# A two-layer mixture-of-experts network: expert 0's rows made by one-hot products

## What is computed

```python
def _moe(x, w_router, router_bias, w_gate, w_up, w_down):
    h = x.reshape(-1, D_MODEL)
    scores = jax.nn.sigmoid(h @ w_router)
    biased = scores + router_bias
    ...                      # the best of 4 groups, and in it the best 2 experts of each token: idx
    wts = jnp.take_along_axis(scores, idx, axis=-1)
    wts = wts / wts.sum(-1, keepdims=True)
    gates = jnp.sum(jax.nn.one_hot(idx, N_EXPERTS) * wts[..., None], axis=1)
    y = jnp.zeros_like(h)
    for e in range(N_EXPERTS):
        he = jax.nn.silu(h @ w_gate[e]) * (h @ w_up[e])
        y = y + gates[:, e:e + 1] * (he @ w_down[e])
    return y
# the layer's output: _layernorm(ALPHA * x + _moe(x, ...), g, b)
```

## Time and profile before

| | us |
|---|---|
| median of 3 runs | 1484.63 (1483.34 to 1486.12) |
| the profiled execution: time | 1496.51 |
| its span | 1494.8 |
| PE matmul busy | 1253.4 (84%) |
| DVE busy | 548.5 (37%) |
| ACT busy | 320.2 (21%) |
| POOL busy | 162.6 (11%) |

### The profile page before, as it was taken

One profiled execution on the slowest core, in us unless ns is written; L12 is line 12 of the kernel. 1 busy time (PEld: TensorE's weight loads), 2 busy tenths in 40 slices (PEclk: granted clock), 3 DMA queues, 4 the chain that ended last, 5 costly groups with the idle time before them and its releaser, 6 DMA issues.

```text
span 1494.8 us, 19415 instructions
## 1 busy us (share of the span) xinstructions
PE 1253.4 (84%) x7442; PEld 758.3 (51%) x7442; DVE 548.5 (37%) x1419; ACT 320.2 (21%) x776; POOL 162.6 (11%) x200
## 2 busy tenths in 40 slices
PE   1999992999972999999998499989997975999940
PEld 0486442454431577778876245546664533454420
DVE  1281354111115357855655334432111362111127
ACT  0101121111111232333332034422220121111111
POOL 0010003000002000012100600004400011000030
PEclk9999995999995999999997679999787986999975
DMA  9238028999924211000000810005403058999642
GB/s 378 80 147 206 0 89 321 380 364 367 349 108 160 113 57 57 0 15 4 3 3 1 255 44 1 1 9 153 137 19 141 1 207 332 353 365 367 260 159 80
DMA packets 68710, 227.56 MB, mean 152 GB/s; under 512 B 7713, under 2 KB 34401, under 8 KB 51969
## 3 DMA queue, kind: packets, MB, share of 16 engines
q1 hardware_dynamic: 41360, 140.95, 26.0%
q0 software_dynamic: 17440, 66.12, 12.7%
q10 hardware_dynamic: 9808, 19.14, 3.5%
HBM read 186.90 MB, written 39.29 MB: 151 GB/s over the span
## 4 chain that ended last, share of the span: by engine, by line
PE 80%; DVE 9%; DMA 6%; issue 3%; ACT 1%; POOL 0%; POOLq 0%; DVEq 0%; SPq 0%; ACTq 0%
PE bank L1152 15%; PE bank L1093 9%; PE bank L1172 7%; PE bank L1298 7%; PE bank L1222 4%; PE bank L1395 3%; PE bank L1240 2%; PE bank L1631 2%; PE bank L1644 2%; PE bank L1653 2%; PE bank L1633 2%; DMA xT<-in_xT_dram 2%; PE bank L1142 2%; DVE acc L2188 2%; PE bank L1583 2%
## 5 line engine op out<-in xcount | busy, mean ns | idle before, releaser
L1093 PE MATMUL bank<-ring,cat 128*128 128x512 f32 (+1 forms) x320 | 143.6, 604 | 9.0 <-DMA ring<-in_stream_dram 7.6
L1152 PE MATMUL bank<-ring,work 128*128 128x512 f32 x256 | 113.9, 597 | 0.0
L1298 PE MATMUL bank<-xT,ring 128*128 128x288 f32 x448 | 110.9, 407 | 0.0
L1093 PEld LDWEIGHTS bank<-ring,cat 128*128 128x128 f32 (+1 forms) x320 | 57.2, 183 | 83.3 <-issue 83.2
L1298 PEld LDWEIGHTS bank<-xT,ring 128*128 128x128 f32 x448 | 84.6, 190 | 24.1 <-issue 1.5
L2168 DVE TENSOR_TENSOR work<-work,bank 128x256 f32<-128x256 f32 x32 | 13.5, 421 | 219.0 <-ACT work L1753 219.0
L1152 PEld LDWEIGHTS bank<-ring,work 128*128 128x128 f32 x256 | 47.9, 192 | 54.2 <-issue 54.2
L1142 PE MATMUL bank<-const,work 128*128 128x128 f32 x256 | 36.1, 290 | 32.9 <-DMA work<-xrows 32.9
L1240 PE MATMUL bank<-ring,xT 128*128 128x512 f32 (+1 forms) x80 | 36.5, 618 | 32.0 <-DMA xT<-in_xT_dram 32.0
L1222 PE MATMUL bank<-xT,ring 128*128 128x288 f32 x256 | 63.1, 407 | 0.0
L1081 PE MATMUL bank<-const,x 128*128 128x128 f32 (+1 forms) x120 | 17.6, 299 | 50.4 <-DVE x L2004 50.4
(11 more groups left out here) (417 smaller groups left out, 2191.5 us busy)
## 6 DMA issues: line engine op xcount, KB each, us to landing
ring<-in_stream_dram SPq DMA_DIRECT2D x71, 1024.0 KB, 8.0
cat<-in_stream_dram SPq DMA_DIRECT2D x16, 1024.0 KB, 8.8
work<-xrows ACTq DMA_DIRECT2D x32, 512.0 KB, 4.9
xT<-in_stream_dram SPq DMA_DIRECT2D x16, 1024.0 KB, 8.1
work<-in_stream_dram SPq DMA_DIRECT2D x16, 1024.0 KB, 9.4
yrows<-work POOLq DMA_DIRECT2D x32, 512.0 KB, 9.0
xrows<-work POOLq DMA_DIRECT2D x1, 8192.0 KB, 27.4
xT<-in_pages_dram SPq DMA_DIRECT2D x33, 128.0 KB
```

Of the source, the lines that this page charges most:

```text
L1093: i = pe.matmul(bank(n)[0:ROWS[tile], :], cat[:, k, tok(tile)], slot(w[k // 4], 4, 512)[:, k % 4, :], start=(k == 0), stop=(k == KC - 1))
L1152: i = pe.matmul(bank(n), xgT[:, e % 2, k, :], sparse_slot(layer, 3 * e + k // 4, 4, 512)[:, k % 4, :], start=(k == 0), stop=(k == KC - 1))
L1298: i = pe.matmul(bank(n + s)[:, 0:nn], slot(w, KC, 256)[:, k, P * (m % 2):P * (m % 2) + P], xT[:, k, a:a + nn], start=(k == 0), stop=(k == ...
```

## The change

1. A new step ("rows", 0) at the end of `FRONT`, with two banks. Behind the flag DVE makes five one-hot masks `of_first`: for each token of a tile 128 columns, which compare its place in expert 0 (`t0`) with the constants 0 to 127 (`slots`, 128 new columns of the constant table) and multiply by whether expert 0 is among its two. PE's `first_rows` multiplies them with `x`, ten f32 products of 512 columns, and ACT and DVE copy the two halves into `xg[:, 0]`. ACT no longer loads expert 0's rows.
2. PE's order begins: rows of 0, gate and up of 0, rows of 1; from e = 1 on it is the old one. ACT's and DVE's orders follow.
3. ACT scales the accumulator, ahead of its copy of the first half; DVE waits for it before it reads the flag.
4. ACT and DVE read the flag behind their copies of the two halves, PE behind `first_rows`. SP waits for both halves and for the row loads of experts 1 and 2 before the four spare weight loads.

```diff
 FRONT = [...
-         ("mT", 4), ("rt", 4), ("pos", 1)]
+         ("mT", 4), ("rt", 4), ("pos", 1), ("rows", 0)]
...
-for kind in ("T0", "T1"):
-    SPARSE_ORDER[0, kind] = len(SPARSE_ORDER)
-for e in range(N_EXP + 1):
+for e, kind in ((0, "T0"), (0, "T1"), (0, "GU"), (1, "T0"), (1, "T1")):
+    SPARSE_ORDER[e, kind] = len(SPARSE_ORDER)
+for e in range(1, N_EXP + 1):
...
+        of_first = view(work, 0, NT, P)
...
                         sp.wait_ge(scattered[layer], 32 * NT)
-                        for i in range(2):
+                        landed_all(sp, f"{layer}.rows0")
+                        for i in (1, 2):
                             sp.wait_ge(xg_loaded[layer][i], 16)
...
+                def first_rows():
+                    n = job(f"{L}rows0")
+                    pe.wait_ge(first_slots, layer + 1)
+                    for half in range(2):
+                        claim(pe, n + half)
+                        for tile in range(NT):
+                            i = pe.matmul(bank(n + half), of_first[0:ROWS[tile], tile, :],
+                                          x[0:ROWS[tile], tile, 512 * half:512 * half + 512],
+                                          start=(tile == 0), stop=(tile == NT - 1))
+                        done(i, n + half)
...
                 turn_rows(0)
-                for e in range(N_EXP + 1):
+                hidden(0)
+                turn_rows(1)
+                for e in range(1, N_EXP + 1):
...
                 router_scores(layer, 1)
+                act.wait_ge(ln_done, (2 * layer + 1) * NT)
+                for tile in range(NT):
+                    r = ROWS[tile]
+                    act.activation(acc[0:r, tile, :], x[0:r, tile, :], ACT.Copy, scale=ALPHA).then_inc(acc_scaled, 1)
+                n = job(f"{L}rows0")
+                take(act, n)
+                give(act.copy(xg[:, 0, 0:512], bank(n)), n)
                 flag = is_crowded(act, layer)
...
-                    for e in range(NXG):
+                    for e in range(1, NXG):
                         load_rows(e)
...
                     dve.tensor_copy(crowded[0:1, 0:1], s1[0:1, 0:1]).then_inc(rows_ready, 1)
+                    for tile in range(NT):
+                        r = ROWS[tile]
+                        i = dve.tensor_scalar(of_first[0:r, tile, :], c("slots", r), t0[0:r, tile, 0:1],
+                                              both[0:r, tile, 0:1], ALU.is_equal, ALU.mult)
+                    i.then_inc(first_slots, 1)
...
                 assign(layer, 1)
-                for tile in range(NT):
-                    r = ROWS[tile]
-                    i = dve.tensor_scalar(acc[0:r, tile, :], x[0:r, tile, :], ALPHA, None, ALU.mult)
-                step(i)
+                n = job(f"{L}rows0") + 1
+                take(dve, n)
+                give(dve.tensor_copy(xg[:, 0, 512:], bank(n)), n)
+                dve.wait_ge(acc_scaled, NT * (layer + 1))
                 flag = is_crowded(dve, layer)
```

More of the change, by code:

```diff
@@ L79, in constant_table @@
     put("ones", np.ones((P, P)))
+    put("slots", np.tile(np.arange(P) * 1.0, (P, 1)))
     put("rowbase", np.tile(P * np.arange(N_EXP) * 1.0, (P, 1)))
@@ L253 @@
     for kind, tile in FRONT:
-        reserve(f"{L}{kind}{tile}", 2 if kind == "mT" else 1)
+        reserve(f"{L}{kind}{tile}", 2 if kind in ("mT", "rows") else 1)
     for e in range(N_EXP):
@@ L540, in program @@
         rows_cleared = sem("rows_cleared")
+        first_slots = sem("first_slots")
+        acc_scaled = sem("acc_scaled")
         scattered = [sem(f"scattered{k}") for k in range(LAYERS)]
@@ L1126, in mixture @@
                         router_logits(at)
+                    elif kind == "rows":
+                        first_rows()
                     else:
@@ L1136, in turn_rows @@
                 def turn_rows(e):
-                    pe.wait_ge(xg_loaded[layer][e % NXG], 16 * (e // NXG + 1))
+                    if e == 0:
+                        landed(pe, job(f"{layer}.rows0"), 2)
+                    else:
+                        pe.wait_ge(xg_loaded[layer][e % NXG], 16 * (e // NXG + (e % NXG > 0)))
                     for g in range(2):
@@ L1736, in mixture, with turned_rows @@
                     act.wait_ge(scattered[layer], 32 * NT)
-                    for e in range(NXG):
+                    for e in range(1, NXG):
                         load_rows(e)
-                    for e in range(-1, N_EXP + 1):
-                        if e + 1 < N_EXP:
-                            n = ejob(layer, e + 1, "T0")
-                            take(act, n)
-                            give(act.copy(xgT[:, (e + 1) % 2, 0:4, :], bank(n, 4, P)), n)
+                    def turned_rows(e):
+                        n = ejob(layer, e, "T0")
+                        take(act, n)
+                        give(act.copy(xgT[:, e % 2, 0:4, :], bank(n, 4, P)), n)
+                    turned_rows(0)
+                    for e in range(N_EXP + 1):
+                        if 0 < e < N_EXP - 1:
+                            turned_rows(e + 1)
                         if e > 0:
@@ L1756, in mixture @@
                                 load_rows(e + NXG)
+                        if e == 0:
+                            turned_rows(1)
                         if e > 0:
@@ L2159, in mixture, with turned_rows @@
                 with dve.Else():
-                    for e in range(-1, N_EXP + 1):
-                        if e + 1 < N_EXP:
-                            n = ejob(layer, e + 1, "T1")
-                            take(dve, n)
-                            give(dve.tensor_copy(xgT[:, (e + 1) % 2, 4:8, :], bank(n, 4, P)), n)
+                    def turned_rows(e):
+                        n = ejob(layer, e, "T1")
+                        take(dve, n)
+                        give(dve.tensor_copy(xgT[:, e % 2, 4:8, :], bank(n, 4, P)), n)
+                    turned_rows(0)
+                    for e in range(N_EXP + 1):
+                        if 0 < e < N_EXP - 1:
+                            turned_rows(e + 1)
                         if 0 <= e < N_EXP:
```

## The result

The changed kernel takes 1499.34 us (median of 4 runs, 1498.7 to 1500.16), the kernel before, beside it, 1484.89 (4 runs): 14.5 us slower, ratio 1.0098, interval 1.0081 to 1.0116. In a second comparison, of 12 runs, it is 1493.74 us against 1484.67: 1.0064 (1.0034 to 1.0093). The forecast was 1491.4, in a range up to 1496.0. Executions of either kernel come in two kinds some 12 us apart, and the profiled execution of before (1496.51 us) was one of the longer kind, while its median was one of the shorter.

The account below looks back on a forecast made before the run. The prediction took PE to bound the kernel, with the expert phase's start deciding its end. Later start of expert 1 (2.4), clock loss (4.2) and longer table (0.2) gave 6.8 us on the 1484.6 median: 1491.4 us, range 1481.5 to 1496.0.

Parts of the forecast that it names:

- Start of the rows: Expert-phase entry: PE may start expert 0's one-hot row products 1.5 us behind the flag write.
- F: Time of DVE's write of the flag `crowded`: 240.30 in layer 0 and 1237.65 in layer 1 before the change.
- Their length: Expert 0's row products on PE: twenty instructions, 8.8 us at full clock, plus 2.1 for starting at 1.2 GHz.
- H: Moment the second half of expert 0's rows is done on PE, forecast at F+12.4 (11.8 to 13.1).
- DVE's wait behind its branch: After DVE's flag branch at the entry: 2.0 us to an instruction packet, 1.7 behind it, 3.7 in all.
- The clock falls in the gap: PE idles 3.4 us before expert 0's product; half clock then costs 2.1 us per layer, 4.2 for both.
- ScalarE's scaling free: Accumulator scaling on ACT: five passes of 1.24 us end 3 us before DVE asks, so cost nothing.
- A: Rival: the clock holds in one or both layers, DVE's fetch remains; 2.6 to 4.7 us slower; chance 0.22.
- B: Rival: DVE goes on at once behind its branch and the clock holds; 2.7 us less, 1481.9; chance 0.20.
- C: Rival: PE reads the flag only after its 20 row instructions; 9.7 us slower, 1494.3; chance 0.10.
- D: Rival: weight stream sets the pace or the new path isn't what delays; no change; chance 0.05.
- the last line of the sum: Whole kernel: the entry's 6.8 us on the profiled execution moves unchanged to the median, 1484.6 to 1491.4 us.

Follow-up runs that it names:

- experiment 6: Kernel before with the accumulator scaled on ScalarE and DVE reading the flag only after PE turned expert 0's first half: 1500.02 us, ratio 1.0091.
- experiment 4: Changed kernel with ACT's and DVE's flag read and branch moved ahead of their copies of expert 0's rows: 1486.75 us, ratio 1.001.
- experiment 1: Kernel before, unaltered, profiled and timed once more: 1484.88 us, ratio 0.9985.
- experiment 2: Kernel before with only the 128 new columns of the constant table: 1484.89 us, ratio 0.9979.
- experiment 9: 17 extra matmuls keeping PE at work in layer 1's latent attention: in the kernel before 1482.04 us (0.9983), in the changed one 1487.07 us (1.0025).
- experiments 1 to 8: Eight follow-ups: the kernel before or the changed kernel, unaltered or with single parts altered; medians from 1482.16 to 1500.02 us.
- experiments 9 to 11: Follow-ups with extra matmuls keeping PE at work, on the kernel before, the changed kernel and variants of both; medians from 1475.22 to 1487.07 us.
- experiment 10: Changed kernel, flag read ahead of the copies, six extra matmuls at the entry: 1478.24 us (0.9965); with latent-attention matmuls too, 1480.71 us (0.9962).

## Why the prediction was wrong

**The entry was right in its mechanism and near in its sum.** Forecast 6.8 us with 0.2 for the table; measured by the marks 7.5 between the two first profiles. Term by term:

- Start of the rows F+1.5: F+1.4. Their length 10.9 with a clock loss of 2.1: 12.35 and 11.78. The clock cost 3.0 and 2.3, and with the clock kept the rows take 9.3, not 8.8, since at and beside the 64-row products the spacing is 0.53 us in place of 0.43. So H is F+13.8 and F+13.2 where F+12.4 stood.
- DVE's wait behind its branch 3.7: 3.54 and 2.86. Its parts, 2.0 to the packet and 1.7 behind it: 1.70 and 1.84 in layer 0, 1.03 and 1.83 in layer 1. The reading of the packets, from the records of PE and q14, held. In layer 1 the shorter wait made up for the later H (the product starts H+4.6, not H+5.35), so that its 2.4 us against 2.6 forecast is in part luck. By the Trainium skill, "Runtime: NRT & Kernel Launch", section "Instruction fetch mechanics", a taken branch whose target lies outside the two resident pages has to fetch it by DMA first; the trace agrees, with these waits and with the packet that goes out 1.8 to 2.0 us ahead of DVE's next instruction in all fourteen waits of this kind (experiment 6), and experiments 4 and 6 show that they go and come with the place of the branch.
- The clock falls in the gap and costs 2.1 in the product: it fell, and the product took 9.6 in place of 7.1, 2.5.
- ScalarE's scaling free, the first scatter near 1 us and worth nothing in the change: 1.07, and nothing.

**The rivals.** A (the clock holds) fell. B fell with the wait; experiment 4 is what it described, and even there the clock did not hold, a condition B had taken for granted. C fell: PE's branch starts at 245.8, some 9 us ahead of the end of the rows. D fell with the marks.

**The step that failed** is the last line of the sum: "All of this is waiting and clock at the same place of every run, so it moves to the median as it is." It put everything outside the entry at nothing. But the clock is not the same in every run: layer 1's attention holds stretches of half clock whose length changes from one execution to the next, by 11 to 12 us in all. The working had noted that the profiled execution stood 0.8% above the median and did not ask what it did there; it held the long stretches, and by their times 29 of 35 executions did not (experiment 1).

What the runs show in its place: by their times the executions of the changed kernel had a long stretch and those of the kernel before did not. All four executions of the changed kernel in the first comparison lay at 1498.7 to 1500.2, and the profiled one of them has the long stretch in the latent attention. Against a profile of before near its median, that of experiment 2 (1485.33 us, only the table longer), its span is 14.8 us longer: 7.6 at the two entries, 9.1 from layer 1's first transposes to its flag, -1.4 between the phase of layer 0 and those transposes, -0.6 ahead of the first output projection. Of the 9.1, 5.8 lie ahead of the first page score (515.7 against 509.9) and 2.9 in the page scores (118.9 against 116.0). The work there is the same, 5674 instructions of PE in both. The latent attention's window of that profile of before, at the same distance behind the transposes as the changed kernel's 852.5 to 872.9, has a clock of 0.67 against 0.50:

```profile
849.90:870.30 20.40, 14.94 (x36) 6.18 (x36) 6.85 (x36) 4.28 (x11) 7.32 (x9) 0.67 0.57 160
```

Between the two first profiles, both with the long stretch there, the difference is 3.7 us in span: +7.5 at the entry, +0.7 at the start of the kernel, -1.6 between the phase of layer 0 and layer 1's first transposes, -3.2 in the page scores, the rest +0.3. Kind against kind in the second comparison it is 5.9, and in the pair of experiment 9, 4.5 (lower eight, 1486.5, against 1482.0). So 6.8 was a fair price of the entry, and the other 7 to 8 us of the 14.5 are the attention's.

**What stays open** is whether the change makes the long kind more frequent. Of the changed kernel 8 of 16 executions were of it, and 10 of 66 of the kernel before in experiments 1 to 8; with the flag early, 4 of 12. That is more than chance would readily give if the executions of a group were independent, and it moves the median. But half of the eight are the four of the first comparison; the second alone has 4 of 12 against 4 of 31, which chance could give, and in experiments 9 to 11 the executions of before (1480.1 to 1497.8) do not part into two clear groups. Why was not found: in the profiles of the long kind the entry marks are those of the short kind (30.5 / 29.9 and 30.6 / 29.7 against 30.2 / 29.7).

## What to carry to other kernels

Before a sum made on one profiled execution is moved to a median, ask what that execution did that the others don't: a profile 0.8% above the median held 12 us lost to half clock in a stage that the sum did not look at. The changed kernel can fall into it too, and then a few executions of each tell little: 14.5 us by four of each, 9.1 by twelve beside thirty-two, 4.5 to 5.9 kind against kind. A flag read and branch is cheap only in the shadow of something longer; moved behind the work that it was hidden beside, it cost 3 to 8 us here, and the clock of the product behind it as well. And ask of a shorter path what the engine idles for on it: with six idle-time products at the entry the old path reached expert 1's product within 0.2 us of the one-hot path with its own in one pair of profiles, and 0.6 and 1.7 us later in the other, with no loss in the median.

## What the hardware showed unexpectedly

- The granted clock falls to half, 1.2 GHz, in stretches where PE is recorded as busy without a gap: 18.00 of 18 us at 0.53 in the paged attention of before. The largest group there is 32 short products of 64 columns (423 ns each). A busy PE in the records is not one at its peak.
- The same program takes these stretches short or long from one execution to the next: 0.53 and 0.98 in the same place.
- The clock fell with gaps of only 0.83 and 0.98 us around a restart whose rows had begun at half clock (experiment 4), and held with the same gaps when PE had been kept at work (experiment 10). So the length of the gap did not decide it between these two; what PE did before differed.
- Behind all fourteen branches of DVE with nothing else to wait for, the next instruction comes 1.81 to 1.97 us after the start of an instruction packet of q14. When that packet goes out varies: 0.96 to 2.91 us behind the branch in thirteen of them (the first packet), 5.83 in the one with the wait of 7.80 us (the second packet, the DMA engines full).
